# Input projections of a hybrid decoder layer: plain fp32 matmuls in place of three fp32r products on split operands

## The chip, the cores and the metric

The kernel runs on one core of one Trainium2 chip. The metric is the device time of one execution in microseconds, from the first to the last instruction of the core with what the runtime puts around them; the time given for a kernel is the median over its runs.

## What is computed

One inference step of a decoder trunk with one layer, for 1024 prompt rows and 8 sample rows of width 1024. All tensors are float32. The part that matters here is the first half of the layer:

```python
h = rmsnorm(x, norm_mix) * (1 + sc1) + sh1      # 1032 x 1024, scale and shift from w_mod
proj = h @ w_in                                  # 1024 -> z, xbc, dt, q, k, v, g_out, gate
xbc, new_buf = causal_conv(xbc, conv_buf, w_conv, b_conv)
xbc = silu(xbc)
...                                              # state-space heads and gated linear attention
out = concatenate([y, o]) @ w_out
x = x + g1 * out
x = x + g2 * peer(h2, ...)                       # 8 heads x 16 experts gathered for every row
```

`w_in` has 1024 rows and these columns: z 1024, xbc 1536, dt 16, q 512, k 512, v 1024, g_out 1024, gate 16. The change concerns the product `h @ w_in` and how its operands are prepared.

## The kernel before

The program is a row of phases. Each is a block of code for every engine, ended by a barrier over all engines: `modulation`, `norm_in`, `projections` (three blocks with a barrier behind each), `mix_sample`, `mix_prompt`, `experts`. Within a block the engines run their own instruction streams in program order and meet through semaphores. The transfers of SyncE (SP) and GpSimd (POOL) go through queues that are served in the order of issue.

**fp32r and the split.** A value cast to fp32r keeps fewer bits of its mantissa. Before the change each operand of the projections is therefore held twice: a high part, which is the value rounded to fp32r (`split_high`, a copy with a cast, line 64), and a low part, which is the value less the high part (`split_low`, line 69). `matmul_split` (lines 74 to 76) makes the product out of three fp32r matmuls, high x high, high x low and low x high, summed in PSUM. The product of the low parts is left out.

**norm_in** makes `h` for tiles of 128 rows (8 tiles of the prompt, one of 8 sample rows) and turns it so that the 1024 channels lie on the partitions. For each tile VectorE multiplies (L335) and adds (L339), TensorE transposes eight 128 x 128 pieces into PSUM (L362), ScalarE copies them out as the high part `hT_high` (L316), and VectorE subtracts this from PSUM for the low part `hT_low` (L69, called `rest` there). Two buffers `h[b]` and two PSUM areas alternate. In the loop VectorE does the split of tile n-1 after the multiply and add of tile n. TensorE's transposes of tile n wait until the split of tile n-2 is done; VectorE's tile n waits until the transposes of tile n-2 are done.

**projections, channel block.** The columns of xbc, q and k make 20 chunks of 128. For each, the weights (`p_w`, 128 x 8 x 128) are the stationary operand and the rows are the moving one, in three thirds of 344 columns; each third sums over 8 slices of the contraction. TensorE makes a chunk into three PSUM banks, two chunks alternate over six banks. ScalarE evacuates (L483), VectorE runs the four-tap convolution on 12 of the chunks (L532 to L539), ScalarE applies silu, GpSimd stores. VectorE splits the weights of chunk c+2 as soon as TensorE has finished with chunk c. SyncE reloads `p_w[b]` once the split of its contents is done, and after the 20 chunks loads the first block of the row weights `p_wt`, the weights `p_ws` of the small projection and three small tensors, and then, once the first block has been split, the second.

**projections, row block.** The columns of z, g_out and v make 6 blocks of 512. Here `hT` is the stationary operand and the weights `p_wt` (128 x 8 x 512, 2 MB) the moving one: 9 tiles of rows, 8 slices each, six PSUM banks in turn, evacuated by ScalarE (L619) and stored by GpSimd (L584). One buffer `p_wt` takes the loads, and is split by VectorE into two pairs of buffers `p_wth`, `p_wtl`.

**projections, small block.** dt and gate, 48 columns with padding (`p_ws`), in three thirds of 344 columns, then the softplus and log-sigmoid work that hangs on them; L678 is a plain fp32 matmul of 16 partitions by 344 columns in it.

Other places that the prediction names: L830 is the output projection in `mix_prompt`, a plain fp32 matmul of 128 x 128 stationary and 512 moving columns, in 8 tiles x 2 halves x 16 slices; L1771 is the weighted sum of gathered experts, L1502 the query projection. Constants: `KD` = 8 slices, `THIRD` = 344, `NT` = 8, `NRT` = 9, `NC` = 20, `P` = 128.

Of the kernel before, what the change touches and what calls it, by code (L numbers as in the profile page):

```python
# [69 lines left out]


def matmul_split(nc, out, lhsT, rhs, start, stop):

    nc.tensor.matmul(out, lhsT[0], rhs[0], start=start, stop=False)  # L74
    nc.tensor.matmul(out, lhsT[0], rhs[1], start=False, stop=False)  # L75
    return nc.tensor.matmul(out, lhsT[1], rhs[0], start=False, stop=stop)  # L76
# [199 lines left out]
def norm_in(g, x, r, hT):  # L276

    nc, io = g.nc, g.io
    with ExitStack() as st:
# [8 lines left out]
        flipped, high, low = sem("n_flipped"), sem("n_high"), sem("n_low")  # L288
# [11 lines left out]
        def each(eng, tile, between=None):  # L300
            for b in range(2):
                tile(b, b, P, False)
            if between:
                between()
            with eng.Fori(1, NT // 2) as i:
                for b in range(2):
                    tile(i * 2 + b, b, P, True)
            tile(NT, 0, NS, True)

        @block.scalar  # L310
        def _(act):
            def tile(n, b, rs, later):
# [3 lines left out]
                nc.scalar.activation(hT[0][:, :, cols], src, ACT.Copy).then_inc(high, 1)  # L316

            each(act, tile)
            act.wait_ge(high, NT + 1)

        @block.vector
        def _(dve):
# [7 lines left out]
            def tile(n, b, rs, later):  # L330
# [9 lines left out]
                if later:  # L340
                    rest(n - 1, 1 - b, P)

            def rest(n, b, rs):

                cols = slice(SEQ, ROWS) if rs == NS else bass.ds(n * P, P)
                src = g.ps[:, 2 * b * 512:2 * b * 512 + KD * P].rearrange("p (k r) -> p k r", r=P)[:, :, 0:rs]
                dve.wait_ge(high, n + 1)
                split_low(nc, hT[1][:, :, cols], hT[0][:, :, cols], src).then_inc(low, 1)

            each(dve, tile, lambda: rest(0, 0, P))  # L350
            rest(NT, 0, NS)
            dve.wait_ge(low, NT + 1)

        @block.tensor
        def _(pe):
            def tile(n, b, rs, later):
                pe.wait_ge(normed, n + 1)
                if later:
                    pe.wait_ge(low, n - 1)
# [9 lines left out]
def projections(g, hT):  # L369

    nc, io = g.nc, g.io
    with ExitStack() as st:
# [4 lines left out]
        wth = [st.enter_context(nc.sbuf_tensor(f"p_wth{b}", [P, KD, 512], F32R)) for b in range(2)]  # L377
        wtl = [st.enter_context(nc.sbuf_tensor(f"p_wtl{b}", [P, KD, 512], F32R)) for b in range(2)]
        wt = sb("p_wt", [P, KD, 512])
        wt_in, wt_high, wt_split = sem("p_wt_in"), sem("p_wt_high"), sem("p_wt_split")  # L380

        ws, wsh, wsl = (st.enter_context(nc.sbuf_tensor(n, [P, KD, 48], dt))
# [1589 lines left out]
```

## Time and profile before

| | |
|---|---|
| median of 3 runs | 4392.82 us (4384.98 to 4402.39) |
| span of the profiled execution | 4384.4 us, 39661 instructions |
| TensorE matmuls busy | 3487.9 us (80%), 11633 |
| TensorE weight loads busy | 1922.7 us (44%) |
| VectorE busy | 2354.8 us (54%) |
| ScalarE busy | 1050.6 us (24%) |
| GpSimd busy | 1348.0 us (31%) |
| DMA | 1269.30 MB, mean 290 GB/s |

The profiled execution is a run of its own. The page gives its span, first to last instruction, 4384.4 us, and no other time for it; it lies at the lower end of the runs. In the rows, PE is TensorE's matmuls, PEld its weight loads, DVE VectorE, ACT ScalarE, POOL GpSimd, SP SyncE. Matmuls overlap in the array's pipeline, so that the mean duration of one is longer than the time from one to the next. PEclk is the granted TensorE clock as a share of its higher level: 1.00 is 2.4 GHz and 0.50 is 1.2 GHz.

### The profile page before, as it was taken

The numbers are of one execution on the slowest core, as the hardware profiler recorded it, in microseconds if no ns is written. First come the engines' busy times: TensorE is split into PE (matmuls) and PEld (weight loads), VectorE is DVE, ScalarE is ACT, GpSimd is POOL, SyncE is SP. The second block draws the span as 40 slices with busy tenths as digits, with TensorE's granted clock in tenths as the row PEclk, the third lists the DMA queues.
The fourth block names the chain that finished last, engine by engine and source line by source line (L and its number), as shares of the span: only waits on it lengthen the run. The fifth ranks groups of instructions, "written<-read, shape, count | busy, mean of one in ns | idle before, by whom it ended". The sixth has DMA issues, their size and how long they took to land.

```text
span 4384.4 us, 39661 instructions
## 1 busy us (share of the span) xinstructions
PE 3487.9 (80%) x11633; PEld 1922.7 (44%) x11633; DVE 2354.8 (54%) x4730; ACT 1050.6 (24%) x3019; POOL 1348.0 (31%) x1232
## 2 busy tenths in 40 slices
PE   7699996469997687786787788778769778877876
PEld 1698774135555342352353344335325324324432
DVE  0651111746663767457546646646755755664574
ACT  1110112123341222222222222222222222222222
POOL 0020110400000343344444443434444444443442
PEclk9799997689998898898899889889889889988988
DMA  7232210642323899999999999999999999999996
GB/s 273 69 103 110 82 61 31 246 165 86 101 72 134 345 374 374 381 384 366 361 389 368 376 375 379 366 370 380 382 384 378 381 374 383 377 375 375 395 382 272
DMA packets 210634, 1269.30 MB, mean 290 GB/s; under 512 B 25875, under 2 KB 51099, under 8 KB 74060
## 3 DMA queue, kind: packets, MB, share of 16 engines
q0 software_dynamic: 159504, 1114.68, 64.3%
q1 hardware_dynamic: 50902, 152.03, 9.9%
q8 instruction: 88, 1.44, 0.1%
q14 instruction: 140, 1.15, 0.1%
HBM read 1218.26 MB, written 48.36 MB: 289 GB/s over the span
## 4 chain that ended last, share of the span: by engine, by line
DMA 26%; PE 25%; issue 8%; ACT 4%; POOL 3%; DVE 3%; POOLq 0%; ACTq 0%; DVEq 0%; SPq 0%
DMA e_buf<-in_experts,e_idx 26%; PE ps L1771 22%; PE ps L1502 3%; POOL e_buf L1738 3%; DVE e_buf L1840 2%; ACT e_wts L1812 2%; ACT e_diag L1816 1%; ACT e_acts L1810 1%; DMA e_buf<-in_experts,e_idxT 0%; DMA r_wq<-in_w_query 0%; POOLq L58 0%; DVE r_work L1590 0%; DVE r_row L1591 0%; DVE r_work L1587 0%; DVE r_pos L1550 0%
## 5 line engine op out<-in xcount | busy, mean ns | idle before, releaser
L1771 PE MATMUL ps<-e_buf,e_diag 128*128 128x512 f32 x4096 | 2026.0, 652 | 638.7 <-ACT e_diag L1816 635.2
L1840 DVE SCALAR_TENSOR_TENSOR e_buf<-e_buf,e_h 128x1024 f32<-128x1024 f32 x1024 | 1248.2, 1227 | 1091.6 <-DMA e_buf<-in_experts,e_idx 1075.2
L1738 POOL DMA_INDIRECT e_buf<-in_experts,e_idx x1024 | 1195.4, 1167 | 1605.1 <-PE ps L1771 1406.3
L1771 PEld LDWEIGHTS ps<-e_buf,e_diag 128*128 128x128 f32 x4096 | 836.0, 210 | 1758.4 <-issue 990.9
L1810 ACT ACTIVATE e_acts<-e_dots 128x4 f32<-128x4 f32 x256 | 52.6, 205 | 2085.0 <-DVE e_buf L1840 2076.4
L1816 ACT ACTIVATE e_diag<-ident,e_wts 128x128 f32<-128x128 f32 x1024 | 327.3, 390 | 27.8 <-ACT e_wts L1812 2.7
L1502 PEld LDWEIGHTS ps<-r_h2T,r_wq 128*128 128x128 f32 x2304 | 269.3, 193 | 34.0 <-issue 34.0
L1502 PE MATMUL ps<-r_h2T,r_wq 128*128 128x128 f32 x2304 | 269.9, 276 | 3.1 <-DMA r_wq<-in_w_query 3.1
L830 PE MATMUL ps<-xo_w_out,xo_catT 128*128 128x512 f32 x512 | 224.5, 592 | 1.7 <-DVE xo_x L863 1.7
L1812 ACT ACTIVATE e_wts<-e_acts,e_gate 128x1 f32<-128x1 f32 x1024 | 218.5, 284 | 9.2 <-ACT e_acts L1810 1.1
L74 PE MATMUL ps<-p_wth,hT_high 128*128 128x512 f32 (+1 forms) x432 | 170.6, 395 | 10.9 <-PEq L413 10.9
L76 PE MATMUL ps<-p_wth,hT_low 128*128 128x512 f32 (+1 forms) x432 | 170.9, 396 | 0.0
L75 PE MATMUL ps<-p_wtl,hT_high 128*128 128x512 f32 (+1 forms) x432 | 170.3, 394 | 0.0
L74 PE MATMUL ps<-hT_high,p_wh 128*128 128x344 f32 x480 | 154.5, 322 | 8.7 <-DVE p_wl L69 8.7
L76 PE MATMUL ps<-hT_high,p_wl 128*128 128x344 f32 x480 | 154.0, 321 | 0.0
L75 PE MATMUL ps<-hT_low,p_wh 128*128 128x344 f32 x480 | 153.9, 321 | 0.0
L830 PEld LDWEIGHTS ps<-xo_w_out,xo_catT 128*128 128x128 f32 x512 | 96.7, 190 | 117.6 <-issue 117.2
L881 POOL DMA_DIRECT2D x_d<-xo_x x8 | 4.3, 542 | 410.9 <-DVE xo_x L863 410.9
L64 DVE CAST p_wth<-p_wt 128x4096 fp32r<-128x4096 f32 x6 | 13.8, 2293 | 198.8 <-PE ps L76 190.6
L584 POOL DMA_DIRECT2D proj_d<-p_ev x54 | 31.6, 585 | 280.6 <-ACT p_ev L619 275.3
L619 ACT ACTIVATE p_ev<-ps 128x512 f32<-128x512 f32 (+1 forms) x54 | 32.2, 596 | 280.0 <-PE ps L76 280.0
L258 PE MATMUL ps<-w_mod_sb,cT 128*9 128x512 f32 x192 | 86.0, 604 | 14.2 <-DMA w_mod_sb<-in_w_mod 8.6
(338 smaller groups left out, 3007.2 us busy)
## 6 DMA issues: line engine op xcount, KB each, us to landing
w_mod_sb<-in_w_mod SPq DMA_DIRECT2D x12, 2048.0 KB, 8.4
e_buf<-in_experts,e_idx POOLq DMA_INDIRECT x1024, 9.1
p_wt<-in_w_rows SPq DMA_DIRECT2D x6, 2048.0 KB
proj_d<-p_ev POOLq DMA_DIRECT2D x48, 256.0 KB, 2.3
x_zgv<-proj_d SPq DMA_DIRECT2D x8, 1536.0 KB
p_w<-in_w_chan SPq DMA_DIRECT2D x20, 512.0 KB, 4.3
r_wq<-in_w_query SPq DMA_DIRECT2D x4, 2048.0 KB, 20.2
xbc_d<-p_res POOLq DMA_DIRECT2D x12, 516.0 KB, 3.0
```

Of the source, the lines that this page charges most:

```text
L74: nc.tensor.matmul(out, lhsT[0], rhs[0], start=start, stop=False)
L75: nc.tensor.matmul(out, lhsT[0], rhs[1], start=False, stop=False)
L76: return nc.tensor.matmul(out, lhsT[1], rhs[0], start=False, stop=stop)
L258: last = nc.tensor.matmul(g.bank(2 + b, rows=NS + 1), cT[:, k, :], w[:, b, k, :], start=(k == 0), stop=(k == KD - 1))
L830: last = g.nc.tensor.matmul(g.bank(cols, rows=rs), self.catT[:, k, 0:rs], self.w[:, k, cols * 512:(cols + 1) * 512], start=(k == 0), stop= ...
L1502: last = nc.tensor.matmul(g.bank(4 + b, cols=P, at=m * P), self.wq[:, b, k, m * P:(m + 1) * P], self.h2T[:, k, :], start=(k == 0), stop=(k ...
L1738: return pool.indirect_dma_start(out=buf[s][:], out_offset=None, in_=io["experts"], in_offset=bass.IndirectOffsetOnAxis(ap=numbers, axis=0 ...
L1771: last = nc.tensor.matmul(g.bank(cols), diag[:, k % RING, :], buf[k % RING][:, D + cols * 512:D + (cols + 1) * 512], start=(k == 0), stop= ...
L1810: ch.step(A(acts[:, ks], dots[:, ks], ACT.Gelu))
L1812: last = A(wts[:, k:k + 1], acts[:, k:k + 1], ACT.Copy, scale=gate[:, k:k + 1])
L1816: A(diag[:, k % RING, :], g.ident[:], ACT.Copy, scale=wts[:, k:k + 1]).then_inc(weighed, 1)
L1840: V.scalar_tensor_tensor(out=down, in0=down, scalar=1.0, in1=row, op0=ALU.mult, op1=ALU.mult, accum_out=out).then_inc(sem, 1)
```

## The change

The activations are kept once, as `hT` in float32, and so are the weights. Every group of three fp32r matmuls becomes one `nc.tensor.matmul` on the fp32 operands. The casts and subtractions on VectorE and the semaphores that went with them are gone from `norm_in` and `projections`, and so is `matmul_split`; `split_high` and `split_low` stay for a use in `mix_sample`. The waits move: TensorE waits for the transfers of the weights themselves; SyncE reloads a channel weight buffer after TensorE has finished with it (`chan`) instead of after its split; `p_wt` becomes two buffers, both loaded behind the last channel weights, and each is reloaded after TensorE has made the nine tiles that use it (`tprod`).

```diff
--- before.py
+++ after.py
@@ -67,13 +67,6 @@
-def matmul_split(nc, out, lhsT, rhs, start, stop):
...
-    nc.tensor.matmul(out, lhsT[0], rhs[0], start=start, stop=False)
-    nc.tensor.matmul(out, lhsT[0], rhs[1], start=False, stop=False)
-    return nc.tensor.matmul(out, lhsT[1], rhs[0], start=False, stop=stop)
@@ -285,7 +278,7 @@
         normed, hchain = sem("n_normed"), sem("n_hchain")
-        flipped, high, low = sem("n_flipped"), sem("n_high"), sem("n_low")
+        flipped, kept = sem("n_flipped"), sem("n_kept")
...
@@ -297,11 +290,9 @@
-        def each(eng, tile, between=None):
+        def each(eng, tile):
...
                 tile(b, b, P, False)
-            if between:
-                between()
...
@@ -313,10 +304,10 @@
                 cols = slice(SEQ, ROWS) if rs == NS else bass.ds(n * P, P)
-                nc.scalar.activation(hT[0][:, :, cols], src, ACT.Copy).then_inc(high, 1)
+                nc.scalar.activation(hT[:, :, cols], src, ACT.Copy).then_inc(kept, 1)
             each(act, tile)
-            act.wait_ge(high, NT + 1)
+            act.wait_ge(kept, NT + 1)
...
@@ -337,26 +328,15 @@
                 nc.vector.tensor_tensor(h[b][0:rs, :], h[b][0:rs, :], shift[kind][0:rs, :], ALU.add).then_inc(normed, 1)
-                if later:
-                    rest(n - 1, 1 - b, P)
...
-            def rest(n, b, rs):
...
-                cols = slice(SEQ, ROWS) if rs == NS else bass.ds(n * P, P)
-                src = g.ps[:, 2 * b * 512:2 * b * 512 + KD * P].rearrange("p (k r) -> p k r", r=P)[:, :, 0:rs]
-                dve.wait_ge(high, n + 1)
-                split_low(nc, hT[1][:, :, cols], hT[0][:, :, cols], src).then_inc(low, 1)
...
-            each(dve, tile, lambda: rest(0, 0, P))
-            rest(NT, 0, NS)
-            dve.wait_ge(low, NT + 1)
...
+            each(dve, tile)
...
         def _(pe):
             def tile(n, b, rs, later):
...
                 if later:
-                    pe.wait_ge(low, n - 1)
+                    pe.wait_ge(kept, n - 1)
...
@@ -374,31 +354,16 @@
-        wth = [st.enter_context(nc.sbuf_tensor(f"p_wth{b}", [P, KD, 512], F32R)) for b in range(2)]
-        wtl = [st.enter_context(nc.sbuf_tensor(f"p_wtl{b}", [P, KD, 512], F32R)) for b in range(2)]
-        wt = sb("p_wt", [P, KD, 512])
-        wt_in, wt_high, wt_split = sem("p_wt_in"), sem("p_wt_high"), sem("p_wt_split")
...
-        ws, wsh, wsl = (st.enter_context(nc.sbuf_tensor(n, [P, KD, 48], dt))
-                        for n, dt in (("p_ws", F32), ("p_wsh", F32R), ("p_wsl", F32R)))
-        ws_in, ws_high, ws_split = sem("p_ws_in"), sem("p_ws_high"), sem("p_ws_split")
+        wt = [sb(f"p_wt{b}", [P, KD, 512]) for b in range(2)]
+        wt_in = [sem("p_wt_in0"), sem("p_wt_in1")]
+        ws, ws_in = sb("p_ws", [P, KD, 48]), sem("p_ws_in")
...
-        def split_rows(dve, i, b):
...
-            dve.wait_ge(wt_in, (i * 2 + b) * 16 + 16)
-            split_high(nc, wth[b][:], wt[:]).then_inc(wt_high, 1)
-            dve.wait_ge(wt_high, i * 2 + b + 1)
-            split_low(nc, wtl[b][:], wth[b][:], wt[:]).then_inc(wt_split, 1)
...
         sb = lambda n, s, dt=F32: chan_mem.enter_context(nc.sbuf_tensor(n, s, dt))
-        wh = [sb(f"p_wh{b}", [P, KD, P], F32R) for b in range(2)]
-        wl = [sb(f"p_wl{b}", [P, KD, P], F32R) for b in range(2)]
         w = [sb(f"p_w{b}", [P, KD, P]) for b in range(2)]
-        w_high, w_split = sem("p_w_high"), sem("p_w_split")
...
@@ -418,15 +383,14 @@
                     for b in range(2):
-                        sp.wait_ge(w_split, i * 2 + b + 1)
+                        sp.wait_ge(chan, i * 2 + b + 1)
                         sp.dma_start(w[b][:], io["w_chan"][bass.ds(i * 2 + b + 2, 1)].squeeze(0)).then_inc(w_in[b], 16)
-                sp.dma_start(wt[:], io["w_rows"][0]).then_inc(wt_in, 16)
+                for b in range(2):
+                    sp.dma_start(wt[b][:], io["w_rows"][b]).then_inc(wt_in[b], 16)
...
                 sp.dma_start(bg[:], io["b_gate"]).then_inc(small_in, 16)
-                sp.wait_ge(wt_split, 1)
-                sp.dma_start(wt[:], io["w_rows"][1]).then_inc(wt_in, 16)
...
@@ -459,21 +423,21 @@
             @block.tensor
             def _(pe):
-                def chunk(b, c):
-                    pe.wait_ge(w_split, c + 1)
+                def chunk(b, nth):
+                    pe.wait_ge(w_in[b], nth * 16 + 16)
...
                         for k in range(KD):
-                            last = matmul_split(nc, g.bank(3 * b + j, cols=THIRD), (wh[b][:, k, :], wl[b][:, k, :]),
-                                                (hT[0][:, k, cols], hT[1][:, k, cols]), k == 0, k == KD - 1)
+                            last = nc.tensor.matmul(g.bank(3 * b + j, cols=THIRD), w[b][:, k, :], hT[:, k, cols],
+                                                    start=(k == 0), stop=(k == KD - 1))
...
                 chunk(0, 0)
-                chunk(1, 1)
+                chunk(1, 0)
...
                         pe.wait_ge(evac, i * 2 + b - 1)
-                        chunk(b, i * 2 + b)
+                        chunk(b, i)
...
@@ -506,22 +470,10 @@
             @block.vector
             def _(dve):
-                def split(i, b, first=False):
...
-                    dve.wait_ge(w_in[b], i * 16 + 16)
-                    if not first:
-                        dve.wait_ge(chan, i * 2 + b - 1)
-                    split_high(nc, wh[b][:], w[b][:]).then_inc(w_high, 1)
-                    dve.wait_ge(w_high, i * 2 + b + 1)
-                    split_low(nc, wl[b][:], wh[b][:], w[b][:]).then_inc(w_split, 1)
...
-                for b in range(2):
-                    split(0, b, True)
...
                     for b in range(2):
-                        split(i + 1, b)
...
@@ -543,16 +495,6 @@
                         assert ch.n == STEPS
-                with dve.Fori(NXBC // 2, NC // 2 - 1) as i:
-                    for b in range(2):
-                        split(i + 1, b)
-                for b in range(2):
-                    split_rows(dve, 0, b)
-                dve.wait_ge(ws_in, 16)
-                split_high(nc, wsh[:], ws[:]).then_inc(ws_high, 1)
-                dve.wait_ge(ws_high, 1)
-                split_low(nc, wsl[:], wsh[:], ws[:]).then_inc(ws_split, 1)
...
@@ -568,8 +510,8 @@
-                        sp.wait_ge(wt_split, i * 2 + b + 2)
-                        sp.dma_start(wt[:], io["w_rows"][bass.ds(i * 2 + b + 2, 1)].squeeze(0)).then_inc(wt_in, 16)
+                        sp.wait_ge(tprod, (i * 2 + b + 1) * NRT)
+                        sp.dma_start(wt[b][:], io["w_rows"][bass.ds(i * 2 + b + 2, 1)].squeeze(0)).then_inc(wt_in[b], 16)
...
@@ -589,7 +531,7 @@
             def _(pe):
                 def block_rows(i, first):
                     for b in range(2):
-                        pe.wait_ge(wt_split, i * 2 + b + 1)
+                        pe.wait_ge(wt_in[b], i * 16 + 16)
...
@@ -597,8 +539,8 @@
                                 rows = slice(t * P, t * P + rs)
-                                last = matmul_split(nc, g.bank(n % 6, rows=rs), (hT[0][:, k, rows], hT[1][:, k, rows]),
-                                                    (wth[b][:, k, :], wtl[b][:, k, :]), k == 0, k == KD - 1)
+                                last = nc.tensor.matmul(g.bank(n % 6, rows=rs), hT[:, k, rows], wt[b][:, k, :],
+                                                        start=(k == 0), stop=(k == KD - 1))
...
@@ -621,13 +563,6 @@
-            @block.vector
-            def _(dve):
-                with dve.Fori(1, 3) as i:
-                    for b in range(2):
-                        dve.wait_ge(tprod, (i * 2 + b - 1) * NRT)
-                        split_rows(dve, i, b)
...
@@ -656,12 +591,12 @@
             @block.tensor
             def _(pe):
                 pe.wait_ge(small_in, 48)
-                pe.wait_ge(ws_split, 1)
+                pe.wait_ge(ws_in, 16)
...
                     for k in range(KD):
-                        last = matmul_split(nc, g.bank(1 + j, rows=48, cols=THIRD), (wsh[:, k, :], wsl[:, k, :]),
-                                            (hT[0][:, k, cols], hT[1][:, k, cols]), k == 0, k == KD - 1)
+                        last = nc.tensor.matmul(g.bank(1 + j, rows=48, cols=THIRD), ws[:, k, :], hT[:, k, cols],
+                                                start=(k == 0), stop=(k == KD - 1))
...
@@ -1896,7 +1831,7 @@
         with ExitStack() as st:
-            hT = [st.enter_context(nc.sbuf_tensor(f"hT_{part}", [P, KD, ROWS], F32R)) for part in ("high", "low")]
+            hT = st.enter_context(nc.sbuf_tensor("hT", [P, KD, ROWS], F32))
...
```

## Rows read from the trace of the kernel before

**Rows 1.** Windows: busy us (and records) of each engine, granted clock, DMA share, GB/s
```profile
155.00:400.00 245.00, 228.45 (x1440) 228.16 (x1440) 114.83 (x144) 34.20 (x33) 40.26 (x68) 0.97 0.33 106
400.00:704.00 304.00, 301.71 (x1296) 229.98 (x1296) 26.88 (x8) 32.13 (x54) 31.06 (x53) 0.99 0.18 70
...
1370.00:4384.00 3014.00, 2336.85 (x6794) 1151.21 (x6794) 1800.58 (x4124) 745.25 (x2525) 1212.48 (x1049) 0.90 0.93 369
```

**Rows 2.** The page: the chain that ended last, shares of the span by line
```profile
DMA e_buf<-in_experts,e_idx 26%; PE ps L1771 22%; PE ps L1502 3%; POOL e_buf L1738 3%; DVE e_buf L1840 2%; ACT e_wts L1812 2%; ACT e_diag L1816 1%; ACT e_acts L1810 1%; DMA e_buf<-in_experts,e_idxT 0%; DMA r_wq<-in_w_query 0%; POOLq L58 0%; DVE r_work L1590 0%; DVE r_row L1591 0%; DVE r_work L1587 0%; DVE r_pos L1550 0%
```

**Rows 3.** Groups of the projections: busy us, mean ns, idle us before and its releaser
```profile
L74 PE MATMUL ps<-p_wth,hT_high 128*128 128x512 f32 (+1 forms) x432 | 170.6, 395 | 10.9 <-PEq L413 10.9
L74 PE MATMUL ps<-hT_high,p_wh 128*128 128x344 f32 x480 | 154.5, 322 | 8.7 <-DVE p_wl L69 8.7
L74 PEld LDWEIGHTS ps<-hT_high,p_wh 128*128 128x128 f32 x480 | 90.9, 189 | 8.8 <-DVE p_wl L69 8.8
L619 ACT ACTIVATE p_ev<-ps 128x512 f32<-128x512 f32 (+1 forms) x54 | 32.2, 596 | 280.0 <-PE ps L76 280.0
L483 ACT ACTIVATE p_raw<-ps 128x1032 f32<-128x1032 f32 x20 | 20.7, 1034 | 172.9 <-PE ps L76 172.9
```

**Rows 4.** Windows: TensorE matmuls alone (the first row with every engine), granted clock
```profile
162.00:170.00 8.00, 7.66 (x38) 7.66 (x39) 2.14 (x5) 0.00 (x0) 0.00 (x0) 0.75 0.40 131
...
170.00:390.00 220.00, 220.00 (x1400) 1.00 0.33 106
...
410.00:700.00 290.00, 290.00 (x1255) 1.00 0.17 65
```

**Rows 5.** Plain fp32 matmuls: groups, runs in the timeline (start, us), min/median/max
```profile
L830 PE MATMUL ps<-xo_w_out,xo_catT 128*128 128x512 f32 x512 | 224.5, 592 | 1.7 <-DVE xo_x L863 1.7
L830 PEld LDWEIGHTS ps<-xo_w_out,xo_catT 128*128 128x128 f32 x512 | 96.7, 190 | 117.6 <-issue 117.2
...
979.23 8.75 PE L830 MATMUL ps<-xo_w_out,xo_catT 128*128 128x512 f32 x20
...
L678 PE MATMUL ps<-p_gT,p_wgu x24: 447/776/937, 726.4 to 745.6; 16*128 16x344 f32 x24
...
726.77 1.60 PE L678 MATMUL ps<-p_gT,p_wgu 16*128 16x344 f32 x5
732.22 3.80 PE L678 MATMUL ps<-p_gT,p_wgu 16*128 16x344 f32 x6 [3.84 <-DVE p_xg L719]
```

**Rows 6.** Timeline of the channel block's start: start us, us, engine, line
```profile
160.33 0.69 DVE L64 CAST p_wh<-p_w 128x1024 fp32r<-128x1024 f32 x1 [6.13 <-DMA p_w<-in_w_chan]
...
162.34 0.66 PE L74 MATMUL ps<-hT_high,p_wh 128*128 128x344 f32 x1 [8.66 <-DVE p_wl L69]
```

**Rows 7.** Timeline of norm_in, tiles 0 to 3 and the last
```profile
121.77 1.28 DVE L335 SCALAR_TENSOR_TENSOR n_h<-x_rows,x_rms,n_scale_p 128x1024 f32<-128x1024 f32 x1
...
124.23 1.28 DVE L335 SCALAR_TENSOR_TENSOR n_h<-x_rows,x_rms,n_scale_p 128x1024 f32<-128x1024 f32 x1
...
124.37 1.97 PE L362 MATMUL ps<-ident,n_h 128*128 128x128 f32 x8 [19.03 <-DVE n_h L339]
...
126.38 1.02 ACT L316 ACTIVATE hT_high<-ps 128x1024 fp32r<-128x1024 f32 x1 [36.95 <-PE ps L362]
...
128.57 1.28 DVE L335 SCALAR_TENSOR_TENSOR n_h<-x_rows,x_rms,n_scale_p 128x1024 f32<-128x1024 f32 x1
...
132.16 1.28 DVE L335 SCALAR_TENSOR_TENSOR n_h<-x_rows,x_rms,n_scale_p 128x1024 f32<-128x1024 f32 x1
...
150.10 1.26 DVE L335 SCALAR_TENSOR_TENSOR n_h<-x_rows,x_rms,n_scale_s 8x1024 f32<-8x1024 f32 x1
...
153.98 0.23 DVE L69 TENSOR_TENSOR hT_low<-ps,hT_high 128x64 fp32r<-128x64 f32 x1 [0.23 <-ACT hT_high L316]
```

**Rows 8.** The page's DMA issues (KB each, us to landing), and p_w's landings
```profile
w_mod_sb<-in_w_mod SPq DMA_DIRECT2D x12, 2048.0 KB, 8.4
...
DMA to landing us min/median/max: 3.1/4.3/6.1
```

## The prediction

> **What bounds the kernel now.** I read the page first, then the table by stretches of time, because the change touches one part of the run only. The table [rows 1] shows the channel projections, 155 to 400 us, the row projections, to 704, and the experts, from 1370; modulation and normalisation lie ahead, the small projection and sequence mixing between. The reader is to see that TensorE is busy 228 of 245 us and 302 of 304 us in the two large stages, at nearly the full granted clock. The expert stage, 69% of the span, is the one that the page's chain lists (expert gathers and L1771, [rows 2]); it has its own limits and starts behind a barrier. So there is no slack later that could take up a longer projection: whatever TensorE's time in the projections changes by, the end changes by.
>
> Inside the two large stages, is it really TensorE? The groups by line [rows 3] give TensorE idle times of 8.7 and 10.9 us, each before the first matmul. ScalarE's evacuations wait 172.9 and 280.0 us for TensorE. VectorE's splits wait for TensorE, not the other way round, apart from the first one. TensorE's stream sets both stages; everything else is cover.
>
> **The new price of a product.** Before: three fp32r matmuls each. Steady stretches [rows 4] hold 1400 of them of 344 columns in 220 us, 0.1571 us each, and 1255 of 512 columns in 290 us, 0.2311 us each. (The 322 and 395 ns of [rows 3] are longer because matmuls overlap in the pipeline; only spacing is a price.) A product costs 0.4714 us at 344 columns and 0.6932 at 512.
>
> After: a plain fp32 product. This kernel already has such products, and two things must be read from them, how many records a product leaves and how far apart these are. Records: the output projection's loops ask for 256 products (8 tiles, 2 halves, 16 slices) and leave 512 records [rows 5]. Two per product. Spacing at 512 columns, at the full clock: a run of 20 takes 8.75 us, so (8.75 - 0.592)/19 = 0.4294 us, with 128-column weights as here. At 344 columns there is one line, L678: its run of 5 takes 1.60 us and the shortest record 0.447, so (1.60 - 0.447)/4 = 0.288 us; and at the lower clock level, where a run of 6 takes 3.80 us and a record at most 0.937, (3.80 - 0.937)/5 = 0.573, twice as much. Scaling 0.4294 by 344/512 gives 0.2885 too. I take 0.288: 0.576 us for a product of 344 columns, 0.859 for one of 512.
>
> So a plain product is dearer than the three it replaces, by 22% and 24%. Break-even would be at 1.6 records per product.
>
> **Channel projections.** 20 chunks x 3 thirds x 8 slices = 480 products: 480 x (0.576 - 0.4714) = +50.2 us. Range: at the bottom 0.286 per record (exactly half of the 0.573 at the lower level), -2 us; at the top the fp32r matmuls' excess over 344 columns at 2.4 GHz, 0.1571 - 0.1433 = 0.014, put on each record, +14 us. L678 feeds 16 partitions instead of 128, but its spacing is what the full-height 0.4294 scales to, so I take it.
>
> **Row projections.** 6 blocks x 9 tiles x 8 = 432 products: 432 x (0.859 - 0.6932) = +71.6 us. The closest row is the output projection, same shape; no bound further than 3 us.
>
> **Small projection.** 24 products of 344 columns: 24 x 0.105 = +2.5 us. The stages start after an idle stretch at the granted clock's lower level (0.75 as the mean of 162 to 170 us, 1.00 after, [rows 4]), and lose a microsecond or two, before as after. I put no change on that.
>
> **The splits that go away.** On VectorE 20 pairs of 0.69 + 1.23 us, 6 of 2.29 + 4.42 and one small pair, all hidden behind TensorE save one: the first. The weights have landed by 160.33, VectorE casts and subtracts, TensorE starts at 162.34 [rows 6]. Now TensorE starts when the weights land: -2.0 us. Everything else of VectorE's is worth nothing while TensorE is the bound.
>
> **Normalisation.** Here VectorE is the bound. Tiles 2 and 3 start at 128.57 and 132.16, 3.59 us apart: three instructions back to back. The first two tiles, with no split between, start 2.46 apart (121.77, 124.23) [rows 7]. Without the split tile 8 starts at 121.77 + 8 x 2.46 = 141.45 instead of 150.10, and the last split, 0.23 us at 153.98, goes too: -8.65 - 0.23 = -8.9 us. What is late next: TensorE's eight transposes per tile span 1.97 us, ScalarE's copy 1.02, both under 2.46; but VectorE's tile n needs the transposes of n-2. Tile 0's were done by 126.38 while tile 2 would start at 126.69: 0.3 us of margin. If that fails somewhere, I lose a few tenths per tile, so this term lies between -5 and -9.5. I take -8.9.
>
> **Transfers moved.** The reload of a channel weight buffer now waits until TensorE has done with the chunk, instead of for the split; its wait and those behind it on SP's queue come later. It then has the next chunk's time, 24 x 0.576 = 13.8 us, and such a load lands in 4.3 us, at most 6.1 [rows 8]. Both row weight blocks (2 MB each) are now issued behind the last of these, when chunk 18 starts, and have 27.6 us; a 2 MB block of the modulation lands in 8.4 us, two make 17. ws and three small loads follow them on the same queue, needed 300 us later. Later row blocks wait for 9 tiles and then have 61.8 us. Cost nothing; uncovered, each chunk would pay its load's excess over 13.8 us. The idle gap of 10.9 us between the two blocks ends with TensorE's sequencer past the barrier [rows 3]; GpSimd's last store and the barrier remain, so I leave it as it is.
>
> **Sum.** +50.2 + 71.6 + 2.5 - 2.0 - 8.9 = +113.4 us. The profiled span of 4384.4 becomes 4497.8. The median of the runs shown, 4392.8, lies 8.4 above the span, and becomes 4506, 2.6% longer.
>
> **The rivals.**
> *One record per product* (the other side). If plain products of these shapes came as one record of 0.288 or 0.4294 us, the stages would take 480 x 0.183 = 88 us, 432 x 0.264 = 114 and 24 x 0.183 = 4 us less than now, and the time would be 4176. It decides below 1.6 records per product. The Trainium skill, Trace Analysis, section "Engine Utilization", notes the array's output rate as halved for FP32_LOW_HIGH; read as the price of a whole fp32 product, that is this rival. The trace agrees with it per record (0.4294 us for 512 columns) but shows two records per product. 2%.
> *Weight loads come out of cover.* Plain loads take 190 ns as the split ones do (189, [rows 3, 5]). If a load stood uncovered before each of the 960 + 864 + 48 records, +356 us: 4862. Partly uncovered, as 0.014 us on each record, +26: 4532. Against it: the 20 records with a load each, 0.4294 us apart. The Trainium skill, TensorE: Matmul & The Clock Gate, section "Weight-path perf modes", turns its fast weight load off for FP32 inputs, which would speak against the change; the trace shows the loads equally long. 5% for the small form, 1% for the full one.
> *The clock falls.* The trace has no stretch of plain matmuls as long as 277 or 371 us. If it were granted only the lower level for a tenth of the 648 us, +65: 4571. Against it: 1.00 in both steady stretches and 0.99 over the whole row stage. 2%.
> *A transfer late.* If loads took over 13.8 us, each microsecond over costs 18 us; at 16 us, +40: 4546. 2%.
> *Normalisation gains little*: 4510 to 4515, inside the range.
>
> **How the numbers follow.** The forecast has 86%, the rivals 12%, and 2% for faster or level in some way I have not seen. The runs shown spread by 9 us around their median; 0.5%, about 22 us, is what a measurement of this kernel can tell from no change. Forecast's terms: channels -2 to +14, rows +-3, normalisation +4, runs +-9. That gives 4492 to 4530; I open it to 4484 to 4533, so that the small form of the second rival is in. Faster 0.03, same 0.02, slower 0.95.
>
> **What would show it.** Two records per product in the projections, 960 of 344 columns 0.288 us apart and 864 of 512 at 0.429; channel stage from about 151 to 430 us, row stage about 373 us long; normalisation's tiles 2.46 us apart; TensorE starting right at the landing of its weights; no wait for p_w or p_wt on TensorE after that; the expert stage as long as before. The prediction is wrong if the record count is below two per product, if spacing at 344 columns is above 0.30, or if TensorE shows idle time inside the stages.

## The result and the profile after

The median goes from 4393.1 us (4384.98 to 4402.39, 4 runs) to 4493.4 (4486.67 to 4501.47, 4 runs): ratio 1.0233, interval 1.0212 to 1.0253. That is 100 us slower, against +113.4 predicted; 4493 lies inside the range of 4484 to 4533. A repetition, further down, gives +105.6 us. The profiled execution of the changed kernel has a span of 4495.0 us, 110.6 above that of before.

The windows of the changed kernel (us; busy time and records of TensorE's matmuls, its weight loads, VectorE, ScalarE, GpSimd; granted clock, DMA share, GB/s). The first is the channel block, the second the row block:

```profile
146.00:441.00 295.00, 279.69 (x960) 183.32 (x960) 63.47 (x98) 34.12 (x33) 37.14 (x68) 0.97 0.24 88
442.00:817.00 375.00, 374.27 (x864) 154.21 (x864) 0.00 (x0) 32.07 (x54) 28.66 (x53) 1.00 0.15 56
```

They answer to [rows 1]. TensorE has fewer records, 960 for 1440 and 864 for 1296, and is busy longer. VectorE has 63 of 115 us of work left in the channel block and none in the row block, and that buys nothing. The groups by line, answering to [rows 3]:

```profile
L542 PE MATMUL ps<-p_wt,hT 128*128 128x512 f32 (+1 forms) x864 | 374.3, 595 | 10.8 <-PEq L378 10.8
L431 PE MATMUL ps<-hT,p_w 128*128 128x344 f32 x960 | 279.7, 455 | 6.1 <-DMA p_w<-in_w_chan 6.1
L431 PEld LDWEIGHTS ps<-hT,p_w 128*128 128x128 f32 x960 | 183.3, 191 | 102.0 <-DMA p_w<-in_w_chan 6.1
L561 ACT ACTIVATE p_ev<-ps 128x512 f32<-128x512 f32 (+1 forms) x54 | 32.2, 596 | 352.5 <-PE ps L542 352.5
```

TensorE idles once ahead of each block and never inside. ScalarE waits for it even longer (352.5 us for 280.0). The spacing comes from TensorE's windows alone, as in [rows 4]:

```profile
170.00:420.00 250.00, 250.00 (x866) 1.00 0.26 93
450.00:800.00 350.00, 350.00 (x814) 1.00 0.16 59
```

250/866 = 0.2887 us at 344 columns, 350/814 = 0.4300 at 512. Normalisation in the timeline (start us, us), VectorE's multiplies of tiles 0 to 3, and then the stage's last copy and the start of the channel block; compare [rows 7] and [rows 6]:

```profile
122.37 1.29 DVE L326 SCALAR_TENSOR_TENSOR n_h<-x_rows,x_rms,n_scale_p 128x1024 f32<-128x1024 f32 x1
...
124.83 1.28 DVE L326 SCALAR_TENSOR_TENSOR n_h<-x_rows,x_rms,n_scale_p 128x1024 f32<-128x1024 f32 x1
...
127.29 1.28 DVE L326 SCALAR_TENSOR_TENSOR n_h<-x_rows,x_rms,n_scale_p 128x1024 f32<-128x1024 f32 x1
...
129.74 1.28 DVE L326 SCALAR_TENSOR_TENSOR n_h<-x_rows,x_rms,n_scale_p 128x1024 f32<-128x1024 f32 x1
...
145.64 0.22 ACT L307 ACTIVATE hT<-ps 128x64 f32<-128x64 f32 x1 [0.37 <-PE ps L342]
146.72 0.83 SPq L383 DMA_DIRECT2D p_w<-in_w_chan  x2
...
151.66 4.70 PE L431 MATMUL ps<-hT,p_w 128*128 128x344 f32 x9 [6.05 <-DMA p_w<-in_w_chan]
```

The tiles are 2.46 us apart to the end, and the first matmul starts at the landing of its weights, 4.9 us after their issue instead of 7.2. Of these 2.3 us the split is 2.0 (160.33 to 162.34 in [rows 6]); the rest is the transfer, which landed 0.3 us sooner.

This table cuts every profiled execution at the same instructions: tile 0's multiply, the issue of the first channel weights, the first matmul of the channel, row and small blocks, the copy of `p_gT`, the transposes of `r_h`, the first and the last expert gather. Lengths in us.

| kernel | normalisation | first weights | channels | rows | small | mixing | gathers |
|---|---|---|---|---|---|---|---|
| before | 33.3 | 7.2 | 239.3 | 310.1 | 13.2 | 654.2 | 2882.8 |
| after | 24.3 | 4.9 | 290.5 | 382.6 | 15.6 | 651.6 | 2880.7 |
| e1 channels plain | 33.3 | 5.1 | 291.7 | 310.6 | 13.5 | 651.3 | 2910.7 |
| e2 rows plain | 33.3 | 7.4 | 239.1 | 382.4 | 12.9 | 650.0 | 2886.4 |
| e3 split back in norm_in | 33.3 | 5.1 | 290.4 | 382.5 | 15.6 | 650.7 | 2892.6 |
| e4 changed again | 24.3 | 4.9 | 290.6 | 382.7 | 15.6 | 646.9 | 2887.9 |
| e5 two products | 33.4 | 6.7 | 180.4 | 210.8 | 10.0 | 651.6 | 2897.8 |
| e6 one product | 33.3 | 6.9 | 173.8 | 112.4 | 5.3 | 650.8 | 2879.5 |
| e7 sixths | 24.4 | 3.5 | 293.3 | 383.3 | 15.9 | 651.7 | 2896.8 |
| e8 twelfths | 24.3 | 5.1 | 830.3 | 382.5 | 15.6 | 650.9 | 2914.5 |
| e9 add on GpSimd | 33.8 | 5.2 | 239.2 | 310.0 | 13.2 | 650.9 | 2894.4 |
| e10 before again | 33.4 | 5.8 | 239.9 | 310.3 | 13.4 | 654.5 | 2897.5 |
| e11 split sixths | 33.4 | 7.0 | 625.6 | 310.8 | 13.7 | 647.5 | 2905.3 |
| e12 wide, then twelfths | 24.4 | 5.4 | 426.5 | 382.9 | 15.7 | 647.4 | 2907.8 |

The channel, row and small blocks repeat to about a microsecond where nothing was changed in them (the plain channel block 290.4 to 291.7 us). The column of the first weights holds a transfer and scatters more: 5.2 to 7.4 us with the split, 3.5 to 5.4 without. Mixing scatters over 8 us and the gathers over 35, whatever the projections are.

### The profile page after: what moved, and what is told of

Same layout as the page of the kernel before. It is cut to its first block, busy times and chain, and to the rows that moved or that the text cites. A ratio compares the mean times of both kernels' runs of the same rounds, so it can differ in the third digit from the quotient of the medians.

```text
span 4495.0 us, 37648 instructions
## 1 busy us (share of the span) xinstructions
PE 3606.2 (80%) x10697; PEld 1795.5 (40%) x10697; DVE 2267.0 (50%) x4667; ACT 1050.7 (23%) x3019; POOL 1358.9 (30%) x1232
## 4 chain that ended last, share of the span: by engine, by line
DMA 25%; PE 24%; issue 8%; POOL 4%; ACT 3%; DVE 3%; POOLq 0%; ACTq 0%; DVEq 0%; SPq 0%
DMA e_buf<-in_experts,e_idx 25%; PE ps L1706 20%; POOL e_buf L1673 4%; PE ps L1437 3%; ACT e_wts L1747 2%; DVE e_buf L1775 2%; ACT e_diag L1751 1%; ACT e_acts L1745 1%; DMA e_buf<-in_experts,e_idxT 0%; POOLq L58 0%; DMA r_wq<-in_w_query 0%; DVE r_pos L1485 0%; DVE r_row L1526 0%; DVE r_work L1525 0%; DVE r_work L1490 0%
## 5 line engine op out<-in xcount | busy, mean ns | idle before, releaser
L1673 POOL DMA_INDIRECT e_buf<-in_experts,e_idx x1024 | 1211.1, 1183 | 1587.2 <-PE ps L1706 1371.7
L542 PE MATMUL ps<-p_wt,hT 128*128 128x512 f32 (+1 forms) x864 | 374.3, 595 | 10.8 <-PEq L378 10.8
L431 PE MATMUL ps<-hT,p_w 128*128 128x344 f32 x960 | 279.7, 455 | 6.1 <-DMA p_w<-in_w_chan 6.1
L542 PEld LDWEIGHTS ps<-p_wt,hT 128*128 128x128 f32 (+1 forms) x864 | 154.2, 180 | 230.5 <-issue 230.5
L431 PEld LDWEIGHTS ps<-hT,p_w 128*128 128x128 f32 x960 | 183.3, 191 | 102.0 <-DMA p_w<-in_w_chan 6.1
L561 ACT ACTIVATE p_ev<-ps 128x512 f32<-128x512 f32 (+1 forms) x54 | 32.2, 596 | 352.5 <-PE ps L542 352.5
L1775 DVE DVE_READ_ACCUMULATOR e_buf<-e_buf,e_h 128x1 f32 x1024 | 84.6, 83 | 0.0
L1481 DVE MAX8 r_v<-r_work 128x8 f32<-128x128 f32 x288 | 62.7, 280 | 40.1 <-ACT r_work L1458 35.2
```

The source lines that it names most:

```text
L431: last = nc.tensor.matmul(g.bank(3 * b + j, cols=THIRD), w[b][:, k, :], hT[:, k, cols], start=(k == 0), stop=(k == KD - 1))
L542: last = nc.tensor.matmul(g.bank(n % 6, rows=rs), hT[:, k, rows], wt[b][:, k, :], start=(k == 0), stop=(k == KD - 1))
L1481: last = V.max(vals[:, u, first:first + 8], src(u))
L1673: return pool.indirect_dma_start(out=buf[s][:], out_offset=None, in_=io["experts"], in_offset=bass.IndirectOffsetOnAxis(ap=numbers, axis=0 ...
L1775: V.scalar_tensor_tensor(out=down, in0=down, scalar=1.0, in1=row, op0=ALU.mult, op1=ALU.mult, accum_out=out).then_inc(sem, 1)
```

## The experiments

The theory: two records per plain product at two array cycles per column, so 22% to 24% more of TensorE's time in stages that TensorE alone bounds, less 9 us of VectorE's in normalisation and 2 at the start. Rivals: the moved transfers or something later hold part of the cost; records are dear for their weight loads.

**e1, the channel block alone.** The moving operand is the high part of `h`, read as fp32; its low part is left out of these products.

```diff
-                            last = matmul_split(nc, g.bank(3 * b + j, cols=THIRD), (wh[b][:, k, :], wl[b][:, k, :]),
-                                                (hT[0][:, k, cols], hT[1][:, k, cols]), k == 0, k == KD - 1)
+                            last = nc.tensor.matmul(g.bank(3 * b + j, cols=THIRD), w[b][:, k, :],
+                                                    hT[0][:, k, cols].bitcast(F32), start=(k == 0), stop=(k == KD - 1))
```

> The kernel before with the channel block alone on plain fp32 matmuls (weights w, moving operand the high part read as fp32; the low part of the activations is left out of these products), its 20 weight splits gone and its weight reloads moved behind the chunk. If the price is two records per product, 960 records 0.288 to 0.289 us apart replace 1440 of 0.157: first matmul to the start of the row block 290.5 us instead of 239.3 (+51), the first matmul 2 us earlier after the weights' issue, normalisation as before, row block 310 us as before; the time is 49 us over the kernel before, about 4442. Rival, the moved reload is part of the cost: TensorE shows idle time inside the block and the block is longer than 960 x 0.289 + 2 us. Rival, the cost lies in the row block alone: no change.

4453.0 us against 4400.2 of before on this chip, ratio 1.0111 (1.0080 to 1.0143). The block is 291.7 us long (+52.4), normalisation and the row block are as before. TensorE has one wait, 6.5 us ahead of the first matmul, and none inside: the moved reload costs nothing. The first matmul comes 5.1 us after the issue of its weights, 2.1 us less than in the first profile of before; but e10 and e9, which still split, have 5.8 and 5.2, so this column alone can't show the gain. It is read from the rows between landing and matmul, where the split takes 2.0 us.

**e2, the row block alone**, the same edit in that block.

> The kernel before with the row block alone on plain fp32 matmuls (stationary operand the high part read as fp32; the low part of the activations is left out of these products), two weight buffers loaded directly and no row weight splits. By two records per product 864 records 0.430 us apart replace 1296 of 0.231: first row matmul to first small matmul 382.6 us instead of 310.1 (+72.5), everything ahead as before; the time is 72 us over the kernel before, about 4466. With the first run the two give +121, and the whole change follows by taking away 9 us of normalisation. Rival, something else of the change holds part of the cost: the two do not add up to it.

4469.4 us, ratio 1.0165 (1.0133 to 1.0196), row block 382.4 us (+72.3). The stage lengths of e1 and e2 add up to the change's: +50.3 (channels with their start) and +72.3 here, against +48.9 and +72.5 in the changed kernel.

**e3, the split back in norm_in.** The changed kernel with VectorE's subtraction for each tile.

```diff
+                if later:
+                    rest(n - 1, 1 - b, P)
...
+                dve.wait_ge(high, n + 1)
+                split_low(nc, hT[1][:, :, cols], hT[0][:, :, cols], src).then_inc(low, 1)
```

> The changed kernel with norm_in as it was before: VectorE again subtracts the copy from PSUM for each tile, into a tensor that nothing reads, with its semaphores and waits. If VectorE is the bound there, the tiles are 3.59 us apart again instead of 2.45 and the stage is 9 us longer (tile 0's multiply to the issue of the first channel weights 33.3 us instead of 24.35); the time is the changed kernel's plus 9, which is 109 to 121 over the kernel before. Rival, transposes or ScalarE set the stage: no change in it.

4520.4 us, ratio 1.0273 (1.0242 to 1.0304). The stage is 33.3 us long, 9.0 more than in the changed kernel, and the tiles are 3.59 us apart again, three instructions of VectorE back to back:

```profile
131.81 1.27 DVE L328 SCALAR_TENSOR_TENSOR n_h<-x_rows,x_rms,n_scale_p 128x1024 f32<-128x1024 f32 x1
133.12 1.22 DVE L332 TENSOR_TENSOR n_h<-n_h,n_shift_p 128x1024 f32<-128x1024 f32 x1
134.26 1.22 DVE L69 TENSOR_TENSOR hT_unread<-ps,hT 128x1024 f32 x1
135.40 1.27 DVE L328 SCALAR_TENSOR_TENSOR n_h<-x_rows,x_rms,n_scale_p 128x1024 f32<-128x1024 f32 x1
```

**e4, the changed kernel again.**

> The changed kernel once more. The profiled executions differ by 112.5 us at the first expert gather; the medians by 100.3 us. If the stages' sum is the whole effect and the medians' difference is scatter of the expert stage, five rounds give a difference of 105 to 115 us and stage lengths equal to 0.3 us; if the change also makes something later shorter by about 10 us in most executions, they give 100 again and the later stages are shorter in this profile too.

4505.9 us against 4400.2, ratio 1.0250 (1.0224 to 1.0276), that is +105.6 us (99 to 121). Every projection stage repeats to 0.2 us.

**e5 and e6, fewer fp32r products.** In e5 the third line of `matmul_split` goes, in e6 the second and third; the products with low parts are left out accordingly, all splits are still made.

```diff
     nc.tensor.matmul(out, lhsT[0], rhs[0], start=start, stop=False)
-    nc.tensor.matmul(out, lhsT[0], rhs[1], start=False, stop=False)
-    return nc.tensor.matmul(out, lhsT[1], rhs[0], start=False, stop=stop)
+    return nc.tensor.matmul(out, lhsT[0], rhs[1], start=False, stop=stop)
```

> The kernel before with two fp32r matmuls for each product instead of three: low x high is left out. If a record's spacing is the price and TensorE sets the stages, 960 records 0.157 us apart and 864 of 0.231 remain: channel block 151 + 2 us long instead of 228, row block 200 + 2 instead of 301, small block 4 us shorter, in all 179 us less than the kernel before, about 4215 to 4225. VectorE needs about 7.3 us for a convolved chunk (187.02 to the end of its last multiply-add, split included) against TensorE's 7.5, so this is the last size at which it is covered. Rival, VectorE's splits and convolution already limit: the channel block is above 160 us, with TensorE waiting for p_wl.

4245.5 us against 4405.2, ratio 0.9636 (0.9593 to 0.9679). The row block's matmuls take 201.8 us from first to last, as the spacing says. The channel block's take 166.8 instead of 153: TensorE waits 4.6 us for VectorE and 7.0 us for ScalarE. And ScalarE there waits for stores:

```profile
PE ps L74 <- PEq L412: 13.3, 1, 13.3
PE ps L74 <- DVE p_wl L69: 12.8, 5, 8.2
PE ps L74 <- ACT p_raw L482: 7.0, 5, 2.2
...
ACT p_raw L482 <- DMA out_conv_s<-p_raw: 44.4, 12, 7.2
```

(Waits: who for whom, us in total, times, longest. The first row is the wait at the barrier between the blocks, the second holds the 8.2 us before the first matmul. `out_conv_s<-p_raw` is the store of a part of `p_raw`.)

> The kernel before with a single fp32r matmul per product, high x high; both other products are left out, all splits are still made. TensorE alone would need 480 x 0.157 = 75 us for the channels and 432 x 0.231 = 100 for the rows. If VectorE's cover ends here as its 7.3 us per convolved chunk says, the channel block takes 12 x 7.3 + 8 x 3.8 = 118 us or more and TensorE waits for p_wl; the row block stays near 100 to 115, since 8.4 us of load and 6.7 of split per block fit under 16.6 by little. Time about 4070 to 4090. Rival, VectorE is still covered: channel block 77 us.

4106.7 us, ratio 0.9321 (0.9294 to 0.9348). The channel block's matmuls span 153.4 us, neither the 77 of TensorE nor the 118 of VectorE: TensorE waits for ScalarE's evacuations and for splits, and ScalarE again for stores:

```profile
PE ps L74 <- ACT p_raw L481: 33.7, 8, 5.7
PE ps L74 <- DVE p_wl L69: 27.1, 7, 8.4
...
ACT p_raw L481 <- DMA out_conv_s<-p_raw: 47.0, 12, 7.7
```

My bound named the wrong engine: VectorE is busy 104.8 of the 153.4 us. The two `p_raw` buffers come free only when GpSimd's stores have landed. By these waits, the ring of evacuation, convolution and store sets the pace once TensorE is quicker, and with three products it was hidden. That is a reading of the waits; no run gave the ring a third buffer. TensorE itself was slower here too: 100.9 us busy for 480 matmuls, where 0.157 us each would be 75, at a mean granted clock of 0.83. The time it stood idle is the other 52.5 us.

**e7 and e8, the same plain products in narrower matmuls** in the channel block, 172 columns in e7 and 86 in e8. The edit of e7 (in e8 the 2 is a 4):

```diff
-                    for j in range(3):
-                        cols = slice(j * THIRD, (j + 1) * THIRD)
+                    for j in range(3 * 2):
+                        n = THIRD // 2
+                        cols = slice(j * n, (j + 1) * n)
```

> The changed kernel with the channel products cut to 172 columns instead of 344: 1920 records instead of 960, the same columns in all, each with its weight load of 128 columns. If a plain record costs two array cycles per column and 2 ns, spacing is 0.145 us and the block takes 281 us, 0 to 4 more than now: time as the changed kernel. Rival, each record costs 0.014 us above its columns: spacing 0.157, block 303 us. Rival, the weight load of 0.19 us cannot lie under a shorter matmul: spacing 0.19, block 365 us.

4515.8 us, ratio 1.0249 (1.0220 to 1.0279), as the changed kernel; block 293.3 us, spacing:

```profile
200.00:300.00 100.00, 100.00 (x687) 1.00 0.21 76
```

0.1456 us for 172 columns. Twice the records and twice the weight loads cost 3 us in all, so the loads are not part of the change's price at 344 and 512 columns.

> The changed kernel with the channel products cut to 86 columns: 3840 records, the same columns in all. By columns alone spacing would be 0.074 us and the block 285 us. If weight loads come out of cover here, the spacing is the one of the 128-column plain records of L1502, 0.122 to 0.127 us, and the block takes 470 to 490 us: 190 to 210 us over the changed kernel. That would give the point at which a load stops being free, and show that the change's 344 and 512 columns lie well above it.

5056.6 us, ratio 1.1477 (1.1400 to 1.1553): the block is 830.3 us long, far beyond the expected 470 to 490. A window of it shows the difference:

```profile
300.00:400.00 100.00, 100.00 (x471) 0.50 0.07 22
```

Spacing 0.2123 us, and the granted clock at its lower level from the first matmul of the block to the last (152.5 to 971.6 us), with no idle time between them.

**e9, an attempt at the 9 us alone.** The kernel before with all its products; the addition of the shift goes to GpSimd, with three buffers for `h` and four PSUM areas.

```diff
+            for n in range(NT + 1):
+                rs, t = rows_of(n), h[n % 3]
+                pool.wait_ge(hchain, n + 1)
+                nc.gpsimd.tensor_tensor(t[0:rs, :], t[0:rs, :], shift[0 if n == NT else 1][0:rs, :],
+                                        ALU.add).then_inc(normed, 1)
```

> The kernel before, with its three fp32r products, but in norm_in the addition of the shift moved from VectorE to GpSimd, three buffers for h and four PSUM areas, and the split of tile n-2 behind the multiply of tile n. VectorE is left with two instructions per tile, 2.4 us; GpSimd's addition takes 1.9 us by its like of 128 x 1024 in the sample phase. If VectorE's three instructions are what the plain product saved there, this version has the same 8 us without paying for it: tile 0's multiply to the issue of the first channel weights 25 to 26 us instead of 33.3, everything behind as before, time 0 to 16 us under the kernel before (8 in the middle, 0.2%). Rival: the two engines slow each other when they run at once, and the stage stays above 30 us.

4399.1 us against 4403.3, ratio 0.9996 (0.9979 to 1.0013): no gain. The stage takes 33.8 us, and the rival's bound of 30 held. From the second half of the stage:

```profile
142.55 1.21 DVE L69 TENSOR_TENSOR hT_low<-ps,hT_high 128x1024 fp32r<-128x1024 f32 x1
142.71 2.35 POOL L318 TENSOR_TENSOR n_h<-n_h,n_shift_p 128x1024 f32<-128x1024 f32 x1 [1.16 <-DVE n_h L338]
143.60 1.02 ACT L309 ACTIVATE hT_high<-ps 128x1024 fp32r<-128x1024 f32 x1 [3.36 <-PE ps L356]
143.68 2.45 DVE L338 SCALAR_TENSOR_TENSOR n_h<-x_rows,x_rms,n_scale_p 128x1024 f32<-128x1024 f32 x1
```

VectorE's multiply takes 2.45 us instead of 1.28 where GpSimd is adding when it starts, so that VectorE is busy without a gap, 3.50 us per tile for 3.59 before, and stays the bound. It is not every instruction of VectorE: the subtraction at 142.55, which reads one input from PSUM, takes its usual 1.21 us beside the same addition. The trace of before has the pair as well: in the sample phase, beside GpSimd's multiplications, VectorE's addition L1401 with both inputs in SBUF takes 2.17 to 2.82 us and L1402, with one input in PSUM, 1.22.

**e10, the kernel before again.**

> The kernel before once more, for its scatter. In all eight kernels run so far the time from the copy of p_gT to the transposes of r_h was 647 to 652 us, and 654.2 in the one profile of before. If that is scatter of its transfers, this profile gives 647 to 654 as well; if the projections' form has an effect on the mixing stage, it gives 654 again. Normalisation 33.3, channel block 239.3, row block 310.1 us as in the first profile, to 0.5 us.

4403.1 us, ratio 0.9995 (0.9982 to 1.0009). Its mixing stage is 654.5 us, the first profile's number again. That fits the rival; but e9, whose projections are those of before, has 650.9, and e11, with fp32r products as well, 647.5. Which of the two it is stays open; it concerns at most 8 us.

**e11, narrow fp32r products**: the kernel before with `j` over six halves of thirds.

> The kernel before with the channel products cut to 172 columns: 2880 fp32r matmuls instead of 1440. By columns at the spacing of 344 (0.157) the block would stay at 228 us; if a record cannot go below the 0.122 to 0.127 us of the 128-column plain records, because each loads 128 weight columns, the block takes 351 to 366 us, 125 to 140 over the kernel before, and three short fp32r records (0.37 us) are then dearer than the two plain ones of this width (0.291 us). Rival, from the run with twelfths: the granted clock stays at the lower level and spacing is 0.213 us, block 613 us, 385 over.

4787.7 us, ratio 1.0870 (1.0836 to 1.0904). The rival of the clock held: 0.50 through the block, spacing 0.213 us, 614.1 us from first to last matmul.

```profile
300.00:500.00 200.00, 200.00 (x939) 0.50 0.11 35
```

**e12, what keeps the clock low.** The first two chunks wide, the rest in twelfths.

```diff
-                chunk(0, 0)
-                chunk(1, 0)
+                chunk(0, 0, 1)
+                chunk(1, 0, 1)
```

> The run with twelfths, but its first two chunks keep matmuls of 344 columns, so that the clock is at its higher level when the 86-column ones begin. In the run with twelfths it was 0.50 from the first matmul to the last of the channel block, without an idle gap, and spacing was 0.213 us. If narrow matmuls only fail to raise the clock, it stays at 1.00 here, their spacing is 0.107 to 0.127 us and the block takes 28 + 18 x 192 x 0.107 to 0.127, that is 400 to 470 us. If they cannot hold it either, it falls back to 0.50 after the second chunk, spacing returns to 0.213 and the block takes about 765 us.

4650.6 us, ratio 1.0555 (1.0495 to 1.0615). The first theory: the clock stays up.

```profile
300.00:500.00 200.00, 200.00 (x1793) 1.00 0.14 51
```

The same 86-column matmuls now stand 0.1115 us apart, and the block takes 426.5 us instead of 830.3. By columns they would need 0.074, so something else sets the spacing. Two lines of the kernel before, plain fp32 at a granted clock of 1.00, tell what:

```profile
1091.20 3.68 PE L1004 MATMUL ps<-x_xdt,x_dec 128*128 128x64 f32 x32
...
1106.06 0.68 PE L1021 MATMUL ps<-x_ref 128*64 128x64 f32 x8
```

Both have 64 moving columns. L1004 loads 128 weight columns for each matmul and stands (3.68 - 0.22)/31 = 0.11 us apart; L1021 loads 64 and stands (0.68 - 0.22)/7 = 0.065 apart, with 0.22 us the shortest record of each. With 128 columns to load, 64 and 86 moving columns stand equally far apart; with 64 to load the spacing nearly halves. So for such short matmuls it goes by the width of the load. The Trainium skill, TensorE: Matmul & The Clock Gate, section "LDWEIGHTS (loading the stationary operand)", puts a load at its columns divided by 1.2, in ns; for 128 columns that makes an estimate of 107 ns. The trace is near it at the higher level (0.1115 us) and shows twice that at the lower (0.2123).

## Why the prediction was right

The mechanism and its parts held, and the runs separate them:

- *Two records per product.* 960 and 864, 0.2887 and 0.4300 us apart, for 0.288 and 0.4294 forecast.
- *Channel projections* +50.2 forecast; +51.2 in the changed kernel, +52.4 in e1. The row of L678, with 16 partitions, was a fair price for 128.
- *Row projections* +71.6 forecast; +72.5, and +72.3 in e2.
- *Small projection* +2.5 forecast; +2.4.
- *Start of the channel block* -2.0 forecast; the 2.0 us between landing and first matmul are gone. The stage itself is 2.3 us shorter, 2.1 in e1; the difference is scatter of the transfer.
- *Normalisation* -8.9 forecast; -9.0, and e3 gives it back. The margin of 0.3 us for the transposes held in every tile: VectorE has no wait between them.
- *Moved transfers* nothing forecast, nothing seen: the weights land in 3.3 us (median) of the chunk's 13.9.
- *Weight loads out of cover*: refuted for these widths by e7. *Clock falls*: refuted; 1.00 in the steady stretches of both blocks. *One record per product*: refuted by the counts. The Trainium skill's halved output rate (Perfetto Trace Analysis, section "Engine Utilization") is what the trace shows per record, 0.4300 us for 512 columns, and not per product, 0.8600.

The stages together are 114.8 us longer, 113.4 forecast. In the two first profiles mixing is then 2.6 us shorter and the gathers 2.1, which with 0.5 us elsewhere gives the spans' difference of 110.6. The medians differ by 100.3 and 105.6 us. The terms behind the projections that I had at nothing scatter more than the spread of the first three runs suggested: mixing 646.9 to 654.5, gathers 2879.5 to 2914.5 us. The second interval, 99 to 121 us, holds the stages' sum, the first (93 to 111) just does not. I put the rest down to this scatter, which is argued and not shown; a systematic few microseconds in mixing can't be excluded. So the total agrees less well than its parts: 4506 was forecast, and 4493 lies near the low end. The sum of the range's upper terms is also wrong: 4506 + 14 + 3 + 4 + 9 is 4536, not 4530. The result lies far from that end, so nothing hangs on it.

Neither form of the full sum over the split operands was improved on. e5 and e6 are quicker than both kernels, but leave products out.

## What to carry to other kernels

Price a matmul's type by records and spacing, not by durations or by the count of calls: where TensorE bounds a stage, one plain fp32 product costs two records at two cycles per column, and three fp32r products at one cycle are 18% to 19% cheaper, in spite of the splits on VectorE, as long as these lie beside the matmuls. Look where the splits do not lie beside matmuls: there, in normalisation, the plain product won 9 us, and handing work from VectorE to GpSimd did not. And when TensorE gets quicker, the next bound need not be the engine with the most work; in e6 the waits point to a ring of two buffers through a store.

## What was unexpected of the hardware

- The same matmuls ran at either clock level for a whole block, by what ran before them: 86-column plain and 172-column fp32r matmuls back to back, each with a load of 128 weight columns, ran at 0.50 for 819 and 614 us after an idle start; the 86-column ones ran at 1.00 for the 18 chunks after two wide ones. Their spacing is 0.2123 against 0.1115 us.
- fp32r matmuls stand 0.014 us (344 columns) and 0.018 us (512) above one cycle per column, plain records 0.002 and 0.003 us above two. The 8-column weight loads do not change it (500.46, 500.69, 500.92 us in the kernel before: 0.231 apart), so it is not the load; the cause was not looked for.
- GpSimd delays some instructions of VectorE and not others (e9, and the sample phase of before). VectorE's multiply with both inputs in SBUF takes 2.45 us instead of 1.28 beside GpSimd's addition, the subtraction that reads PSUM 1.21 as ever. Whether GpSimd is slowed in turn is not shown: its addition takes 2.35 us, but also 2.33 in the last tile, where only that subtraction runs beside it; its multiplication of the same size in the sample phase of before takes 1.91 (median of 8).
